# Seven RMS norms of a fused two-block kernel: from TensorE sums and transposes to VectorE sums and rows read back from memory

## The chip, the cores and the metric

The kernel runs on one core of one Trainium2 chip. The metric is device time in microseconds (us), the median of several runs. TensorE is called PE below, VectorE DVE, ScalarE ACT, GpSimd POOL, SyncE SP.

## The reference, cut to what is computed

Two blocks run one after the other on x, 512 tokens of width 1024, float32.

```
h = x
h = h + mamba2_mixer(rms_norm(h, g_pre[0]))           # SSM block
ckv, k_rope = split(rms_norm(h, g_kv_in) @ w_dkv)      # latent K/V, norm "kv"
ckv = rms_norm(ckv, g_ckv)                             # norm "ck", width 256
cq, gate = split(rms_norm(h, g_pre[1]) @ w_in)         # the same h: norm "kv" again
q = rms_norm(cq, g_q) @ w_uq                           # norm "cq", width 384
h = h + attention(q, k, v) * silu(gate) @ w_out        # 16 heads, causal
h = rms_norm(h, g_final)                               # norm "first" (sum "m1")
h = h + 0.5 * swiglu(rms_norm(h, ffn1_norm))           # norm "both" (sums "m1", "m2")
h = h + hybrid_mixer(rms_norm(h, mix_norm))            # norm "mx"
h = h + 0.5 * swiglu(rms_norm(h, ffn2_norm))           # norm "f2"
return rms_norm(h, final_norm)

rms_norm(x, g) = x * rsqrt(mean(x * x, axis=-1) + 1e-6) * g
```

A norm needs one number for each of the 512 tokens, the reciprocal root of a mean over features.

## The kernel before

Activations lie transposed: features on the 128 partitions, the 512 tokens along the row, eight tiles of 128x512 for width 1024 (`H`). Each float32 operand is split into a high part (`wr`, `XR`) and a low part (`wl`, `XL`), and each product is three matmuls (`three`, L771 to L773): of one 128x512 output tile with 1024 features, 24 matmuls. One weight load of 128x1024 is a **unit**, and mostly one unit is one output tile.

Weights flow in one fixed order of units. SP loads unit j into `raw` (4 buffers), ACT copies it to `wr` (L1221, `hi()`, 3 buffers, so it waits until PE is through with unit j-3), DVE writes the low part `wl` (L1569, `lo()`), PE begins unit j when `wl` is there. The queues of ACT and DVE are written out by hand and run in order. In the loop step of tile i, DVE first calls `lo()` for unit i+2, then does what that step has of other work, and last evicts tile i from PSUM. ACT's step i begins with `hi()` for unit i+2 and ends with the activation of what DVE evicted. So the next `hi()` stands behind this step's eviction on DVE, and the next `lo()` behind that `hi()`.

A norm is applied after the product: the weights are multiplied with the raw h times its gain, and the eviction multiplies with the row of reciprocal roots, `RS`, 128x512, the same row on every partition. The row is made so:

- ACT squares each tile of h (`square`), DVE adds the squares into `ACC` or `TB` (`fold`, L1579).
- PE sums over the partitions: `sums(key)` (L785), four matmuls of `ACC` with a column of ones, 128x4 in bank 3. It stands inside a tile, ahead of that tile's last triple.
- DVE turns the 128x4 sums into means (`root`, L1611) and takes the root by three Newton steps on 128x4 (`newton`, L1595 to L1605). For "ck" and "cq" the root is taken by POOL (L2318 to L2327).
- PE spreads the four columns into a row on all partitions: `spread(key)` (L795), four transposes of a broadcast column.
- DVE copies the row to `RS` (`row_scale`, L1618), or to `RK` for "ck" (L1916). The row of "first" is read from bank 3 where it is used.

In the attention's inputs (`latents`): 4 units `kv_down` (the last triple of one has the sum "kv"), then 11 tiles `mla_in`, steps i = 0 to 10, then 2 units for v. Step 0 evicts the two latent tiles to `craw` with `RS`, step 2 holds "ck", step 8 the sum of "cq", step 10 its row. In the first feed-forward stage (44 tiles, steps j), `fold` m1 and m2 end in step 0, both sums and both roots stand in step 1, and from `READY[0] = 3` on tiles are evicted: step 3 takes tiles 0 to 3 at once. In the second, `READY[1] = 1`. In the second mixer, `mix_v` has tokens on partitions and ACT scales by the 128x4 column `RN` (L1475); its output tiles of the second half share bank 4 with those of the first.

Of the kernel before, what the change touches and what calls it, by code (L numbers as in the profile page):

```python
# [16 lines left out]
D = 1024  # L17
# [20 lines left out]
READY = [3, 1]  # L38
# [284 lines left out]
def build_in(nc, dr, out, top):  # L323
# [28 lines left out]
    gain2 = sb("gain2", [128, KT])  # L352
    PB = [top.enter_context(nc.psum_tensor(f"pb{i}", [128, S], F32)) for i in range(8)]
# [57 lines left out]
    UPS.append([low(f"ffn1UP{i}", [128, S], F32, ph) for i in range(2)])  # L411
    ph.close()
# [28 lines left out]

    def col(name, i=0):
        at = cols[name][0] + i
        return vec[:, at:at + 1]
# [13 lines left out]
    s_sq, s_fold, s_sums, s_sv = sem("s_sq"), sem("s_fold"), sem("s_sums"), sem("s_sv")  # L458
    s_groot, s_root, s_spread, s_rs, s_vroot = [sem("s_" + n) for n in ("groot", "root", "spread", "rs", "vroot")]
# [47 lines left out]
    spreads = {n: i for i, n in enumerate(("x", "g0", "g1", "g2", "g3", "kv", "ck", "cq", "both", "first", "mix", "f2",  # L507
                                           "fin0", "fin1"))}
    sums_no = {n: i + 1 for i, n in enumerate(("x", "g0", "g1", "g2", "g3", "kv", "ck", "cq", "m1", "m2", "mx", "f2",
                                               "fin0", "fin1"))}  # L510
    rooted = {n: (s_root, i + 1) for i, n in enumerate(("x", "kv", "first", "both", "mx", "f2", "fin0", "fin1"))}
    rooted.update({n: (s_groot, i + 1) for i, n in enumerate(("g0", "g1", "g2", "g3", "ck", "cq"))})
    rooted["mix"] = rooted["mx"]
    root_of = {"both": RQ, "ck": RT, **{n: GN for n in ("g0", "g1", "g2", "g3", "cq")}}
    taken = {n: i + 1 for i, n in enumerate(("x", "g0", "g1", "g2", "g3", "kv", "ck", "cq", "m", "m2", "mx", "f2", "fin0",
                                            "fin1"))}
# [71 lines left out]
    bk.place("sum kv", 3, (s_sums, sums_no["kv"]), (s_sv, taken["kv"]))  # L588
    ring = Ring([4, 5, 6, 0, 1])
    for i, n in enumerate(MLA_ORDER):  # L590
        bk.place(("mi", n), ring.next(), whole("mla_in", n), (s_craw, 3 + n) if n < 3 else (s_sg, n - 2))
        if i == 0:
            bk.place("spread kv", 3, (s_spread, spreads["kv"] + 1), (s_rs, 2))
        if i == 2:
            bk.place("sum ck", 7, (s_sums, sums_no["ck"]), (s_sv, taken["ck"]))
        if i == 5:
            bk.place("spread ck", 7, (s_spread, spreads["ck"] + 1), (s_rk, 1))
        if i == 8:
            bk.place("sum cq", 3, (s_sums, sums_no["cq"]), (s_sv, taken["cq"]))
        if i == 10:  # L600
            bk.place("spread cq", 3, (s_spread, spreads["cq"] + 1), (s_tq, 1))
# [47 lines left out]
    def place_ffn(f):  # L649
        ring = Ring([0, 1, 2, 4, 5, 6, 7] if f == 0 else [1, 2, 4, 5, 6, 7, 0])  # L650
        name = f"ffn{f + 1}"
        for j in range(2 * FT):
            up, t = j % 2, j // 2
            bk.place((name, up, t), ring.next(), whole(name + "_in", FT * up + t),
                     (s_up if up else s_ga, FT * f + t + 1))
            if f == 0 and j == 1:
                bk.place("sum m", 3, (s_sums, sums_no["m2"]), (s_sv, taken["m2"]))
            if f == 0 and j == READY[0]:
                bk.place("spread both", 3, (s_spread, spreads["both"] + 1), (s_rs, 3))
            if f == 0 and j == READY[0] + 2:  # L660
                bk.place("spread first", 3, (s_spread, spreads["first"] + 1), (s_hn, 8))
            if f == 1 and j == 0:
                bk.place("sum f2", 3, (s_sums, sums_no["f2"]), (s_sv, taken["f2"]))
            if f == 1 and j == READY[1]:
                bk.place("spread f2", 3, (s_spread, spreads["f2"] + 1), (s_rs, 5))
# [12 lines left out]
    for hf in range(2):  # L678
        for i in range(4):
            bk.place(("vg", hf, i), ((4, 5, 6, 7), (0, 1, 2, 4))[hf][i], whole("mix_v", 4 * hf + 3),  # L680
                     (s_vg, 4 * hf + i + 1))
        if hf == 0:
            bk.place("sum mx", 3, (s_sums, sums_no["mx"]), (s_sv, taken["mx"]))
        else:
            bk.place("spread mix", 3, (s_spread, spreads["mix"] + 1), (s_rs, 4))
# [67 lines left out]
    def _(e):  # L753
# [165 lines left out]
        def latents():  # L919
            for k in range(4):  # L920
                r, l = take("kv_down", k)
                for t in (2 * k, 2 * k + 1):
                    w.wait_ge(s_xlo, tile_x(1, t))
                    for n in range(3):
                        o = opened(("kd", n)) if t == 0 else PB[n]
                        if t == 7 and n == 2:
                            sums("kv")
# [4 lines left out]
            def side(i):  # L932
                if i == 0:
                    spread("kv")
                if i == 2:
                    sums("ck")
                if i == 5:
                    spread("ck")
                if i == 8:
                    sums("cq")  # L940
                if i == 10:
                    spread("cq")

            for i, n in enumerate(MLA_ORDER):
                tile_of(("mi", n), "mla_in", n, XR, XL, ready=(s_xlo, 16), side=lambda t: side(i) if t == 7 else None)
# [120 lines left out]
        def ffn(f):  # L1066
            name = f"ffn{f + 1}"

            def side(j):
                if f == 0 and j == 1:  # L1070
                    sums("m1", 0, "m")
                    sums("m2", 4, "m")
                if f == 0 and j == READY[0]:
                    spread("both")
                if f == 0 and j == READY[0] + 2:
                    spread("first")
                if f == 1 and j == 0:
                    sums("f2")
                if f == 1 and j == READY[1]:
                    spread("f2")  # L1080

            for j in range(2 * FT):
                tile_of((name, j % 2, j // 2), name + "_in", FT * (j % 2) + j // 2, XR, XL,
                        ready=(s_xlo, 32 if f == 0 else 48), side=lambda t: side(j) if t == 7 else None)
# [64 lines left out]
        def second_mixer():  # L1149
            for hf in range(2):  # L1150
                for k in range(4):
                    r, l = take("mix_v", 4 * hf + k)
                    for t in (2 * k, 2 * k + 1):
                        c = slice(512 * (t % 2), 512 * (t % 2) + 512)
                        if t == 6 and hf == 0:
                            sums("mx")
                        if t == 6 and hf == 1:
                            spread("mix")
# [47 lines left out]
    def _(e):  # L1206
# [148 lines left out]
        def latents():  # L1355
# [11 lines left out]
            for i, n in enumerate(MLA_ORDER):  # L1367
# [7 lines left out]
                if n < 3:  # L1375
                    w.wait_ge(s_craw, 3 + n)
                    e.activation(CQ[:, 0, n, :], craw[2 + n], ACT.Copy, scale=col("g_q", n)).then_inc(s_cqhi, 1)
                    w.wait_ge(s_sums, sums_no["ck"])
# [170 lines left out]
    def _(e):  # L1549
# [40 lines left out]
        def then(sem_, last):  # L1590
            return sem_ if last else c.up()

# [271 lines left out]
        def latents():  # L1864
            for k in range(4):
# [5 lines left out]
                if k == 1:  # L1871
                    fold("kv", 7)
                if k == 3:
                    for i in range(6):
                        x_lo(2, i, H[:, i, :], col("g_pre1", i))
                    root("kv")
            for t in range(6, KT):
                x_lo(2, t, H[:, t, :], col("g_pre1", t))
            for i, n in enumerate(MLA_ORDER):
                lo()  # L1880
                if i == 0:
                    row_scale("kv")
                    w.wait_ge(s_rs, 2)
# [28 lines left out]
                if i == 2:  # L1912
                    sum_of("ck", 256)
                if i == 5:
                    w.wait_ge(*bk.full["spread ck"])
                    e.tensor_copy(RK[:, :], PB[7][:, :]).then_inc(s_rk, 1)  # L1916
                if i == 8:
                    sum_of("cq", 384)
                if i == 10:
                    w.wait_ge(*bk.full["spread cq"])  # L1920
                    w.wait_ge(s_krope, 3)
                    e.tensor_tensor(TQ[:, :], PB[3][:, :], TB[:, :], ALU.mult)
                    e.tensor_tensor(TA[64:128, :], PB[3][64:128, :], TA[64:128, :], ALU.mult)
                    e.tensor_copy(TS[96:128, :], PB[3][96:128, :]).then_inc(s_tq, 1)
# [12 lines left out]
            for hf in range(2):  # L1937
                lo()

        def project(h):  # L1940


            for kind, g, i in pieces[h + 1]:
# [19 lines left out]
                else:  # L1963
                    o = PB[bk.bank["k", g, i]]
                    w.wait_ge(*bk.full["k", g, i])
                    w.wait_ge(s_rk, 1)
# [59 lines left out]
        def ffn_side(f, j):  # L2026
# [3 lines left out]
            if f == 0 and j == 1:  # L2030
                w.wait_ge(s_sums, sums_no["m2"])
                e.tensor_scalar(SV[:, :], PB[3][:, 0:4], 1.0 / D, EPS, ALU.mult, ALU.add).then_inc(s_sv, 1)
                w.wait_ge(s_sv, taken["m"])
                newton(RN, s_root)
                w.wait_ge(*rooted["first"])
                e.tensor_tensor(RP[:, :], RN[:, :], RN[:, :], ALU.mult).then_inc(c.up(), 1)
                w.wait_ge(c.h, c.n)
                e.tensor_tensor(RP[:, :], RP[:, :], PB[3][:, 4:8], ALU.mult).then_inc(s_sv, 1)
                w.wait_ge(s_sv, taken["m2"])
                e.tensor_scalar(SV[:, :], RP[:, :], 1.0 / D, EPS, ALU.mult, ALU.add).then_inc(c.up(), 1)  # L2040
                w.wait_ge(c.h, c.n)
                newton(RQ, None)
                w.wait_ge(c.h, c.n)
                e.tensor_tensor(RQ[:, :], RQ[:, :], RN[:, :], ALU.mult).then_inc(s_root, 1)
            if f == 0 and j == READY[0]:
                row_scale("both")
            if f == 0 and READY[0] + 2 <= j < READY[0] + 6:
                w.wait_ge(*bk.full["spread first"])
                for n in (2 * (j - READY[0] - 2), 2 * (j - READY[0] - 2) + 1):
                    e.scalar_tensor_tensor(out=H[:, n, :], in0=H[:, n, :], scalar=col("g_final", n), in1=PB[3][:, :],  # L2050
                                           op0=ALU.mult, op1=ALU.mult).then_inc(s_hn, 1)
            if f == 1 and j == 0:
                fold("f2", 7)
                root("f2")
            if f == 1 and j == READY[1]:
                row_scale("f2")

        def ffn(f, gain):
            name = f"ffn{f + 1}"
            for j in range(2 * FT):  # L2060
                lo()
                ffn_side(f, j)
                for i in ffn_turn(f, j):
# [4 lines left out]
                    w.wait_ge(s_rs, 3 if f == 0 else 5)  # L2068
# [17 lines left out]
        def second_mixer():  # L2086
            for hf in range(2):
                for k in range(4):
# [3 lines left out]
                    if k == 3 and hf == 0:  # L2092
                        root("mx")
# [355 lines left out]
```

## Time and profile before

| | |
|---|---|
| median of 3 runs | 1813.01 us (1812.87 to 1813.54) |
| span of the profiled execution | 1810.9 us |
| granted TensorE clock | 0.999 |
| PE / weight loads / DVE / ACT / POOL busy | 99% / 80% / 57% / 41% / 4% |
| DMA engines busy, mean rate | about a third, 94 GB/s |

The span runs from the first to the last instruction; the time of a run has some 2 us around it. Busy shares are averages over all stages. Matmuls are pipelined, so PE's time is read from the starts of its matmuls, not from their durations.

### The profile page before, as it was taken

What the parts mean: (1) busy time and instruction counts of PE and PEld (TensorE: products, weight loads), DVE (VectorE), ACT (ScalarE), POOL (GpSimd) and SP (SyncE); (2) the same over time, 40 slices, a digit from 0 to 9 for tenths busy, and PEclk for the clock granted to TensorE, in tenths of its full rate; (3) what the DMA queues carried; (4) which work ended last, traced back from release to release, by engine and by line L of the source; (5) the groups of instructions that cost most, each with busy time, mean ns of one, the idle gap of its engine ahead of it and who ended that gap; (6) DMA issues with size and microseconds to landing.
All of it is one profiled execution on the core that took longest, in us unless ns stands there. A gap on an engine that the chain in (4) does not pass through costs nothing.

```text
span 1810.9 us, 21230 instructions
## 1 busy us (share of the span) xinstructions
PE 1799.0 (99%) x8390; PEld 1454.8 (80%) x8390; DVE 1039.5 (57%) x1502; ACT 735.5 (41%) x1202; POOL 71.1 (4%) x137
## 2 busy tenths in 40 slices
PE   9999999999999999999999999999999999999998
PEld 7777777888766788888888888888888888888887
DVE  8899986566687565444333356554444544444333
ACT  5788885433477532322222332223222322322221
POOL 1002021001210000000000000000000000000000
PEclk9999999999999999999999999999999999999999
DMA  5466562232211223333333323233333333323331
GB/s 177 93 108 112 112 107 83 98 93 93 72 36 36 82 81 105 93 93 100 93 100 101 119 81 95 95 95 102 94 98 100 94 93 102 97 93 93 102 99 56
DMA packets 50578, 170.85 MB, mean 94 GB/s; under 512 B 5808, under 2 KB 8368, under 8 KB 50480
## 3 DMA queue, kind: packets, MB, share of 16 engines
q1 hardware_dynamic: 47376, 161.44, 28.5%
q0 software_dynamic: 2240, 7.34, 4.8%
q8 instruction: 67, 1.10, 0.2%
q10 hardware_dynamic: 864, 0.72, 0.1%
q14 instruction: 31, 0.25, 0.0%
HBM read 167.31 MB, written 2.16 MB: 94 GB/s over the span
## 4 chain that ended last, share of the span: by engine, by line
PE 93%; DVE 4%; ACT 1%; issue 1%; DMA 0%; SPq 0%; DVEq 0%; ACTq 0%
PE pb L771 28%; PE pb L773 27%; PE pb L772 27%; PE pb L990 2%; PE pb L882 2%; PE pb L1019 1%; PE pb L995 1%; PE pb L1163 1%; PE pb L1165 1%; PE pb L1164 1%; PE pb L785 1%; DVE CV L1741 0%; DVE wl L1569 0%; PE pb L1173 0%; DMA raw<-in_ssm_in 0%
## 5 line engine op out<-in xcount | busy, mean ns | idle before, releaser
L771 PE MATMUL pb<-XR,wr 128*128 128x512 f32 x1584 | 625.4, 395 | 0.6 <-DVE wl L1569 0.4
L773 PE MATMUL pb<-XR,wl 128*128 128x512 f32 x1584 | 617.0, 390 | 0.0
L772 PE MATMUL pb<-XL,wr 128*128 128x512 f32 x1584 | 616.9, 389 | 0.0
L1569 DVE TENSOR_TENSOR wl<-raw,wr 128x1024 fp32r<-128x1024 f32 (+1 forms) x297 | 358.3, 1206 | 351.0 <-ACT wr L1221 349.9
L1221 ACT ACTIVATE wr<-raw 128x1024 fp32r<-128x1024 f32 (+1 forms) x295 | 305.3, 1035 | 299.1 <-PE pb L773 273.6
L771 PEld LDWEIGHTS pb<-XR,wr 128*128 128x128 f32 x1584 | 297.4, 188 | 65.8 <-issue 3.9
L773 PEld LDWEIGHTS pb<-XR,wl 128*128 128x128 f32 x1584 | 297.2, 188 | 62.6
L772 PEld LDWEIGHTS pb<-XL,wr 128*128 128x128 f32 x1584 | 297.6, 188 | 60.2 <-issue 0.2
L771 PE MATMUL pb<-ffn2HR,wr 128*128 128x512 f32 (+1 forms) x198 | 72.7, 367 | 0.0
L772 PE MATMUL pb<-ffn2HL,wr 128*128 128x512 f32 (+1 forms) x198 | 72.3, 365 | 0.0
L773 PE MATMUL pb<-ffn2HR,wl 128*128 128x512 f32 (+1 forms) x198 | 72.3, 365 | 0.0
L771 PE MATMUL pb<-ffn1HR,wr 128*128 128x512 f32 x176 | 68.5, 389 | 0.0
L772 PE MATMUL pb<-ffn1HL,wr 128*128 128x512 f32 x176 | 68.5, 389 | 0.0
L773 PE MATMUL pb<-ffn1HR,wl 128*128 128x512 f32 x176 | 68.5, 389 | 0.0
L1230 ACT ACTIVATE SQ<-H 128x512 f32<-128x512 f32 x34 | 21.5, 631 | 92.3 <-DVE H L1752 47.6
L1741 DVE SCALAR_TENSOR_TENSOR CV<-U,vec,CV 128x512 f32<-128x512 f32 x72 | 54.1, 752 | 2.5
L1460 ACT ACTIVATE ffn2HR<-ffn2UP 128x512 fp32r<-128x512 f32 x22 | 13.9, 633 | 97.1 <-DVE ffn2UP L2075 97.1
L2340 POOL TENSOR_TENSOR H<-H,RS 128x256 f32<-128x256 f32 x2 | 1.4, 730 | 1278.1 <-ACT RS L1542 1278.1
L1460 ACT ACTIVATE ffn1HR<-ffn1UP 128x512 fp32r<-128x512 f32 x22 | 13.9, 633 | 90.4 <-DVE ffn1UP L2075 90.4
L771 PE MATMUL pb<-YR,wr 128*128 128x512 f32 x128 | 50.0, 391 | 0.0
L1828 DVE TENSOR_TENSOR LL<-LL,CB 128x1024 f32<-128x1024 f32 (+1 forms) x64 | 48.4, 819 | 2.5 <-ACT LL L1290 2.5
L773 PE MATMUL pb<-YR,wl 128*128 128x512 f32 x128 | 49.8, 389 | 0.0
(354 smaller groups left out, 2317.6 us busy)
## 6 DMA issues: line engine op xcount, KB each, us to landing
raw<-in_ffn_in SPq DMA_DIRECT2D x88, 512.0 KB, 3.5
raw<-in_mix_in SPq DMA_DIRECT2D x48, 512.0 KB, 3.5
raw<-in_ssm_in SPq DMA_DIRECT2D x40, 512.0 KB, 4.3
raw<-in_ffn_out SPq DMA_DIRECT2D x32, 512.0 KB, 3.5
DB<-cum POOLq DMA_DIRECT2D x28, 256.0 KB, 8.6
raw<-in_ffn_out SPq DMA_DIRECT2D x16, 384.0 KB, 3.2
raw<-in_mla_in SPq DMA_DIRECT2D x11, 512.0 KB, 3.3
raw<-in_ssm_out_a SPq DMA_DIRECT2D x8, 512.0 KB, 3.2
```

The source lines that it names most:

```text
L771: e.matmul(o, r, xr, start=first, stop=False)
L772: e.matmul(o, r, xl, start=False, stop=False)
L773: return e.matmul(o, l, xr, start=False, stop=last)
L785: m = e.matmul(o[:, at + i:at + i + 1], accs[key][:, 128 * i:128 * i + 128], ones[:, 0:1], start=True, stop=True)
L882: m = e.matmul(y[64 * p:64 * p + 64, 128 * k:S], XD[:, k, j, 64 * p:64 * p + 64], LL[q % 2][:, p, 512 * k:512 * k + S - 128 * k], start=k ...
L990: e.matmul(o[:, at:at + n], q[:, 128 * i:128 * i + 128], kh[:, 0:n], start=True, stop=False)
L1221: e.activation(wr[j % NS][:, 0:width(j)], raw[j % NR][:, 0:width(j)], ACT.Copy).then_inc(s_hi, 1)
L1230: e.activation(SQ[i][:, :], src, ACT.Square, scale=gain).then_inc(s_sq, 1)
L1460: e.activation(HRS[f][:, t, :], UPS[f][t % 2][:, :], ACT.Copy).then_inc(s_hhi, 1)
L1569: e.tensor_tensor(wl[j % NS][:, 0:width(j)], raw[j % NR][:, 0:width(j)], wr[j % NS][:, 0:width(j)].bitcast(F32), ALU.subtract).then_inc(s_ ...
L1741: e.scalar_tensor_tensor(out=cv, in0=u[:, k:k + S], scalar=col("conv_w", 4 * ch + k), in1=cv, op0=ALU.mult, op1=ALU.add).then_inc(then(s_c ...
L1828: m = e.tensor_tensor(x, x, CB[g % 2][:, OFF[k]:OFF[k] + d].unsqueeze(1).to_broadcast([128, 2, d]), ALU.mult)
```

## The change

Seven norms ("kv", "ck", "cq", "first", "both", "mx", "f2") no longer use PE. DVE transposes `ACC` in 32x32 blocks, sums over 32, gathers the four partition groups into 32x64 and sums again: 32x16, of which partition p, column b is token 32b+p. The root is taken on this tile on DVE, a 32x32 transpose makes 16 rows of 32 tokens of it, and POOL's queue writes them (2 KB) to a scratch tensor `rows` in HBM and reads them back as a row on 128 partitions (256 KB), for "ck" and "mx" also as a 128x4 column. The norms of x, of the SSM groups and of the end stay as they were. READY[1] goes from 1 to 3.

```diff
-READY = [3, 1]
+READY = [3, 3]
+    rows = nc.dram_tensor("rows", (len(row_no), 16, 32), F32, kind="Internal").ap()
+    def row_of(key):
+        return rows[row_no[key]:row_no[key] + 1].rearrange("a b c -> a (b c)").to_broadcast([128, S])
+    def columns_of(key):
+        return rows[row_no[key]].rearrange("(c q) j -> (q j) c", q=4)
...
 # PE: latents, ffn, second_mixer
-                            sums("kv")
-            def side(i):  # sums/spread of kv, ck, cq at i = 0, 2, 5, 8, 10
-            def side(j):  # sums of m1, m2, f2; spread of both, first, f2
-                            sums("mx")
-                            spread("mix")
...
 # ACT
-                    w.wait_ge(s_groot, 5)
+                    w.wait_ge(s_cols, 16)
-                    w.wait_ge(*rooted["mx"])
+                    w.wait_ge(s_cols, 32)
...
 # DVE
+        def mean_row(key, n, scratch):
+            w.wait_ge(s_fold, sq.folded[key, sizes[key] - 1])
+            e.transpose(scratch[:, :], accs[key][:, :]).then_inc(c.up(), 1)
+            w.wait_ge(c.h, c.n)
+            e.tensor_reduce(QP[:, :], scratch[:, :].rearrange("p (b j) -> p b j", j=32), AX.X, ALU.add).then_inc(c.up(), 1)
+            w.wait_ge(c.h, c.n)
+            for q in range(4):
+                m = e.tensor_copy(scratch[0:32, 16 * q:16 * q + 16], QP[32 * q:32 * q + 32, :])
+            m.then_inc(c.up(), 1)
+            w.wait_ge(c.h, c.n)
+            e.tensor_reduce(QV[0:32, :], scratch[0:32, 0:64].rearrange("p (q b) -> p b q", q=4), AX.X,
+                            ALU.add).then_inc(s_red, 1)
+            w.wait_ge(*reduced[key])
+            if n is not None:
+                e.tensor_scalar(QV[0:32, :], QV[0:32, :], 1.0 / n, EPS, ALU.mult, ALU.add).then_inc(c.up(), 1)
+                w.wait_ge(c.h, c.n)
+        def row_root(dst):  # first guess and three Newton steps as newton(), on 32x16: 10 instructions
+        def send_row(key, src):
+            k = row_no[key]
+            if k >= 2:
+                w.wait_ge(s_rowout, 16 * (k - 1))
+            e.transpose(QT32[k % 2][0:32, :], src[0:32, :]).then_inc(s_row4, 1)
+        def row_norm(key, n):
+            mean_row(key, n, SQ[0])
+            row_root(QA)
+            send_row(key, QA)
...
                 if k == 1:
                     fold("kv", 7)
+                    row_norm("kv", D)
...
-                    row_scale("kv")
-                    w.wait_ge(s_rs, 2)
+                    w.wait_ge(*row_at["kv"])
...
                 if i == 2:
-                    sum_of("ck", 256)
+                    row_norm("ck", 256)
+                if i == 7:
+                    row_norm("cq", 384)
...
 # steps 5, 8 and 10 lose their copies; TQ, TA, TS are made behind the loop, from OT:
+            w.wait_ge(*row_at["cq"])
+            e.tensor_tensor(TQ[:, :], OT[:, :], TB[:, :], ALU.mult)
...
             if f == 0 and j == 1:
-                ... two newtons on 128x4
+                mean_row("m1", D, SQ[0])
+                row_root(QA)
+                send_row("first", QA)
+                e.tensor_tensor(QW[0:32, :], QA[0:32, 0:16], QA[0:32, 0:16], ALU.mult).then_inc(c.up(), 1)
+                mean_row("m2", None, SQ[1])
+                ... QV * QW, then the mean: two instructions
+                row_root(QB)
+                e.tensor_tensor(QB[0:32, 0:16], QB[0:32, 0:16], QA[0:32, 0:16], ALU.mult).then_inc(c.up(), 1)
+                send_row("both", QB)
-            if f == 0 and j == READY[0]:
-                row_scale("both")
...
             if f == 1 and j == 0:
                 fold("f2", 7)
-                root("f2")
+                row_norm("f2", D)
...
                     if k == 0 and hf == 0:
                         fold("mx", 7)
+                    if k == 1 and hf == 0:
+                        row_norm("mx", D)
 # POOL
+        def row_out(key):
+            k = row_no[key]
+            w.wait_ge(s_row4, k + 1)
+            e.dma_start(rows[k], QT32[k % 2][0:16, :]).then_inc(s_rowout, 16)
+        def row_in(key, dst):
+            w.wait_ge(s_rowout, 16 * row_no[key] + 16)
+            e.dma_start(dst[:, :], row_of(key)).then_inc(row_at[key][0], 16)
+        def cols_in(key, dst):
+            with nc.allow_non_contiguous_dma(reason="a column of four from a row"):
+                e.dma_start(dst[:, :], columns_of(key)).then_inc(s_cols, 16)
+        row_out("kv"); row_in("kv", RS); row_out("ck"); row_in("ck", RK); cols_in("ck", RT)
+        row_out("cq"); row_in("cq", OT)
         ... POOL's own low parts (POOL_LO)
+        row_out("first"); row_out("both"); row_in("both", RS); row_in("first", RX)
+        row_out("mx"); cols_in("mx", RN); row_in("mx", RS); row_out("f2"); row_in("f2", RS)
```

## Rows read from the trace of the kernel before

**Rows 1.** The page: PE's busy time, and the chain that ended last, by engine.
```profile
PE 1799.0 (99%) x8390; PEld 1454.8 (80%) x8390; DVE 1039.5 (57%) x1502; ACT 735.5 (41%) x1202; POOL 71.1 (4%) x137
...
PE 93%; DVE 4%; ACT 1%; issue 1%; DMA 0%; SPq 0%; DVEq 0%; ACTq 0%
```

**Rows 2.** Timeline of PE at "kv": start us, us, engine, line, instruction.
```profile
397.49 0.39 PE L773 MATMUL pb<-XR,wl 128*128 128x512 f32 x1
...
398.53 0.48 PE L771 MATMUL pb<-XR,wr 128*128 128x512 f32 x1
398.85 0.39 PE L772 MATMUL pb<-XL,wr 128*128 128x512 f32 x1
...
403.19 0.39 PE L773 MATMUL pb<-XR,wl 128*128 128x512 f32 x1
403.72 0.50 PE L771 MATMUL pb<-XR,wr 128*128 128x512 f32 x1
...
404.29 0.40 PE L773 MATMUL pb<-XR,wl 128*128 128x512 f32 x1
...
404.88 0.47 PE L771 MATMUL pb<-XR,wr 128*128 128x512 f32 x1
```

**Rows 3.** Grouped by form, DVE: the nearest shapes to the new instructions.
```profile
L1984 DVE TENSOR_REDUCE st<-pb 128x1 f32<-128x512 f32 x16 | 11.1, 692 | 4.1 <-PE pb L991 3.8
...
L1794 DVE COPY TB<-SZ 32x128 f32<-32x128 f32 x4 | 0.9, 221 | 0.1
```

**Rows 4.** Timeline of DVE: the roots of ffn1, first and last of 25 instructions.
```profile
645.05 0.16 DVE L2032 TENSOR_SCALAR SV<-pb 128x4 f32<-128x4 f32 x1 [0.67 <-PE pb L785]
...
649.79 0.16 DVE L2044 TENSOR_TENSOR RQ<-RQ,RN 128x4 f32<-128x4 f32 x1
```

**Rows 5.** DMA issues on SP's queue: count, KB, median us to landing.
```profile
BB<-in_sgu_b SPq DMA_DIRECT2D x1, 512.0 KB, 4.6
...
cum<-CM SPq DMA_DIRECT2D x1, 64.0 KB, 1.5
```

**Rows 6.** The 28 loads of DB, 256 KB each, on POOL's queue.
```profile
DMA to landing us min/median/max: 7.9/8.6/11.4
```

**Rows 7.** Timeline of DVE in the attention's inputs, from "kv" to step 4.
```profile
388.26 0.68 DVE L1579 TENSOR_TENSOR ACC<-ACC,SQ 128x512 f32<-128x512 f32 x1
...
396.91 4.06 DVE L1587 SCALAR_TENSOR_TENSOR XL<-H,vec,XR 128x512 fp32r<-128x512 f32 x6
...
406.10 0.69 DVE L1886 TENSOR_TENSOR PP<-pb,RS 128x512 f32<-128x512 f32 x1
...
426.08 1.23 DVE L1569 TENSOR_TENSOR wl<-raw,wr 128x1024 fp32r<-128x1024 f32 x1 [1.72 <-ACT wr L1221]
...
432.30 1.23 DVE L1569 TENSOR_TENSOR wl<-raw,wr 128x1024 fp32r<-128x1024 f32 x1 [1.72 <-ACT wr L1221]
```

**Rows 8.** Timeline of PE: first matmuls of tiles 5, 6 (mla_in), 6 (ffn1).
```profile
428.39 0.39 PE L771 MATMUL pb<-XR,wr 128*128 128x512 f32 x1
...
434.29 0.39 PE L771 MATMUL pb<-XR,wr 128*128 128x512 f32 x1
...
668.36 0.39 PE L771 MATMUL pb<-XR,wr 128*128 128x512 f32 x1
```

**Rows 9.** Timeline of DVE in ffn1: steps 1, 3 and 4.
```profile
643.15 1.22 DVE L1569 TENSOR_TENSOR wl<-raw,wr 128x1024 fp32r<-128x1024 f32 x1
...
656.51 0.69 DVE L1618 COPY RS<-pb 128x512 f32<-128x512 f32 x1 [2.73 <-PE pb L795]
...
664.64 1.23 DVE L1569 TENSOR_TENSOR wl<-raw,wr 128x1024 fp32r<-128x1024 f32 x1 [0.33 <-ACT wr L1221]
```

**Rows 10.** Timeline of POOL: one instruction of the root of "ck".
```profile
426.24 1.12 POOL L2322 TENSOR_TENSOR GW<-RT 128x4 f32<-128x4 f32 x1
```

**Rows 11.** Timelines in mix_v: DVE's second low part, ACT's first gelu.
```profile
1001.65 1.22 DVE L1569 TENSOR_TENSOR wl<-raw,wr 128x1024 fp32r<-128x1024 f32 x1 [1.83 <-ACT wr L1221]
...
1017.67 0.69 ACT L1475 ACTIVATE VG<-pb,RN 128x512 f32<-128x512 f32 x1 [0.51 <-PE pb L1165]
```

More of the change, by code:

```diff
@@ L352, in build_in @@
     gain2 = sb("gain2", [128, KT])
+    QP, QV, QS, QW = [sb(n, [128, 16]) for n in ("QP", "QV", "QS", "QW")]
+    QA, QB = [sb(n, [128, 32]) for n in ("QA", "QB")]
+    QT32 = [sb(f"QT32{i}", [128, 32]) for i in range(2)]
     PB = [top.enter_context(nc.psum_tensor(f"pb{i}", [128, S], F32)) for i in range(8)]
@@ L411, in build_in @@
     UPS.append([low(f"ffn1UP{i}", [128, S], F32, ph) for i in range(2)])
+    RX = low("RX", [128, S], F32, ph)
     ph.close()
@@ L440, in build_in @@
     cum = nc.dram_tensor("cum", (1, 4, 32, 128), F32, kind="Internal").ap()
+    row_no = {n: i for i, n in enumerate(("kv", "ck", "cq", "first", "both", "mx", "f2"))}
+    rows = nc.dram_tensor("rows", (len(row_no), 16, 32), F32, kind="Internal").ap()
[3 more added lines that the diff above has]
+        return rows[row_no[key]].rearrange("(c q) j -> (q j) c", q=4)
     def col(name, i=0):
@@ L458, in build_in @@
     s_sq, s_fold, s_sums, s_sv = sem("s_sq"), sem("s_fold"), sem("s_sums"), sem("s_sv")
+    s_red, s_row4, s_rowout, s_rows, s_cols = [sem("s_" + n) for n in ("red", "row4", "rowout", "rows", "cols")]
+    s_rowx = sem("s_rowx")
     s_groot, s_root, s_spread, s_rs, s_vroot = [sem("s_" + n) for n in ("groot", "root", "spread", "rs", "vroot")]
@@ L506, in build_in @@
     conv_no = {n: i for i, n in enumerate(convs)}
[L507 to L516, printed above, removed]
+    spreads = {n: i for i, n in enumerate(("x", "g0", "g1", "g2", "g3", "fin0", "fin1"))}
+    sums_no = {n: i + 1 for i, n in enumerate(("x", "g0", "g1", "g2", "g3", "fin0", "fin1"))}
+    rooted = {n: (s_root, i + 1) for i, n in enumerate(("x", "fin0", "fin1"))}
+    rooted.update({n: (s_groot, i + 1) for i, n in enumerate(("g0", "g1", "g2", "g3"))})
+    root_of = {n: GN for n in ("g0", "g1", "g2", "g3")}
+    taken = {n: i + 1 for i, n in enumerate(("x", "g0", "g1", "g2", "g3", "fin0", "fin1"))}
+    reduced = {n: (s_red, i + 1) for i, n in enumerate(("kv", "ck", "cq", "m1", "m2", "mx", "f2"))}
+    row_at = {n: (s_rows, 16 * i + 16) for i, n in enumerate(("kv", "ck", "cq", "both", "mx", "f2"))}
+    row_at["first"] = (s_rowx, 16)
     def whole(name, n):
@@ L655, in place_ffn @@
                      (s_up if up else s_ga, FT * f + t + 1))
-            if f == 0 and j == 1:
-                bk.place("sum m", 3, (s_sums, sums_no["m2"]), (s_sv, taken["m2"]))
-            if f == 0 and j == READY[0]:
[L659 to L665, printed above, removed]
         for c in range(KT if f == 0 else KT - 1):
@@ L930, in latents @@
                 m.then_inc(s_unit, 1)
-            def side(i):
[L933 to L945, printed above, removed]
+            for n in MLA_ORDER:
+                tile_of(("mi", n), "mla_in", n, XR, XL, ready=(s_xlo, 16))
             w.wait_ge(s_cklo, 2)
@@ L1067, in ffn @@
             name = f"ffn{f + 1}"
-            def side(j):
[L1070 to L1080, printed above, removed]
             for j in range(2 * FT):
                 tile_of((name, j % 2, j // 2), name + "_in", FT * (j % 2) + j // 2, XR, XL,
-                        ready=(s_xlo, 32 if f == 0 else 48), side=lambda t: side(j) if t == 7 else None)
+                        ready=(s_xlo, 32 if f == 0 else 48))
             for c in range(KT if f == 0 else KT - 1):
@@ L2067, in ffn @@
                     w.wait_ge(*bk.full[name, up, t])
-                    w.wait_ge(s_rs, 3 if f == 0 else 5)
+                    w.wait_ge(*row_at["both" if f == 0 else "f2"])
                     if not up:
@@ L2181, in _ @@
         e.memset(RQ[:, :], 0.0).then_inc(s_warm, 1)
+        for q in (QA, QB):
+            e.memset(q[:, :], 0.0).then_inc(c.up(), 1)
         for i in range(2):
@@ L2334, in _ @@
                             wr[j % NS][:, 0:width(j)].bitcast(F32), ALU.subtract).then_inc(s_lo, 1)
+        row_out("first")
+        row_out("both")
+        row_in("both", RS)
+        row_in("first", RX)
+        row_out("mx")
+        w.wait_ge(s_rowout, 16 * row_no["mx"] + 16)
+        cols_in("mx", RN)
+        row_in("mx", RS)
+        row_out("f2")
+        row_in("f2", RS)
         w.wait_ge(s_prescale, len(POOL_OUT))
```

86 lines of the change are left out of this document (32 added, 54 removed).

## The prediction, made before the changed kernel was run

> **What bounds the kernel now.** I read the page first. PE is busy for 99% of the span and makes up 93% of the chain that ended last; DVE has 4% of it [rows 1]. So the time falls by what PE no longer does, and rises by each stretch in which PE waits. Three things have then to be found: what a sum and a spread cost PE, how long the new work holds DVE, and by how much DVE may be late before PE runs dry. The first is in the timeline of PE, where the starts of matmuls have to be looked at: in an undisturbed tile they are 0.227 us apart (tile 6 starts 5.90 us behind tile 5, less 0.45 for the spread between them, over 24 [rows 8]). The last is in the timeline of DVE beside the first matmul of each tile: `lo()` for unit i+2 is called in step i and has to end before tile i+2 begins.
>
> **What PE is spared.** At "kv" the matmul ahead of the sum starts at 397.49 and the one behind it at 398.53: 1.04, less the usual 0.23, is 0.81. The next comes 0.32 later and not 0.23, another 0.09 [rows 2]. A sum costs 0.90. The spread: 404.29 to 404.88 is 0.59, less 0.23 is 0.36, with the same 0.09 behind it 0.45. There are seven sums and seven spreads: 6.3 + 3.15. And PE waits once for the low parts XL, which stand behind the root of "kv" on DVE: 403.19 to 403.72 is 0.53, 0.30 too many [rows 2]; with the root gone from there this wait goes. Together 9.8 us.
>
> **What one norm costs DVE.** No row shows a DVE transpose. Below, it can't be under the fixed part of a small instruction, 0.16 [rows 4]; above, two passes would be twice the 0.69 of a 128x512 reduction [rows 3]. It moves the same 128x512 as that reduction, so I take 0.69. The reduction of the transposed tile reads as much as L1984: 0.69. Each has some 0.03 behind it for the wait on its own result. The four copies of 32x16 are at most 0.22 each, which is what 32x128 takes [rows 3], and at least some 0.06: I take 0.12, together 0.5. The 32x64 reduction 0.23. Dependent instructions on 128x4 follow each other at (649.79 - 645.05)/24 = 0.1975 [rows 4], and 32x16 is hardly more: mean 0.2, ten for the root 1.98, last transpose 0.2. **R = 4.55 us** in all; with the transpose and copies at their bounds 3.9 to 5.6. For "first" and "both" the chain is two partition sums (2.17 each), two roots (1.98 each) and seven small instructions (1.4): **C = 9.7 us**, 8.4 to 12.
>
> **What the way through memory takes.** L is the time from the end of DVE's last transpose until the row has landed. The nearest row for reading it back is DB, 256 KB from a few addresses onto 128 partitions through the same queue: 7.9 to 11.4 [rows 6]. BB, one 4 KB row to 128 partitions from SP, 512 KB, took 4.6 [rows 5]. Writing 2 KB is at least the 1.5 of cum [rows 5]. Our 256 KB from 2 KB lie between half of BB and DB. I take 5.0 for the read and 2.2 for the write: **L = 7.2 us**, from 4.5 (1.5 and something over half of BB) to 14 (the slowest DB and 2.6). POOL also shares something with DVE: an instruction on 128x4 which otherwise takes 0.20 took 1.12, from 426.24 to 427.36 [rows 10], while DVE ran `lo()` from 426.08 to 427.31 [rows 7]. Behind the end of C, DVE runs two `lo()`; that part of L is in my 2.2 with 0.5. The Trainium skill, page "SBUF — State Buffer", section "SBUF: two separate sides", says that two SBUF inputs shut POOL out only where POOL's instruction reads SBUF, and that the descriptors of POOL's DMAs are held up by the performance modes of DVE. By that, those 0.5 us fall away and the sum below comes out 0.5 lower; the stretched instruction in the trace reads SBUF and agrees with the first half, and no row here shows the second.
>
> **Where the norm "ck" stands: step 2 of the attention's inputs.** First, DVE is earlier than before. In the new kernel "kv" is done behind its fold, from 388.9 to 393.5, in a pause of DVE, and the row lands at 393.5 + 7.2 = 400.7. The six XL end at 400.97 [rows 7], two more and one `lo()` need 0.68 x 2 + 1.23 (less overlap), and `craw` can start at 403.55 where before it was 406.10: the eleven instructions of the root and the copy to RS no longer lie between. That is 2.55 us earlier, and it is carried on, since from here ACT and DVE wait for each other and not for PE (the pause in front of `lo()` in steps 3 and 4 is one for ACT [rows 7]). Then step 2 adds R less the 0.2 of the old mean: +4.35. So `lo()` of step 4, which ended at 432.30 + 1.23 = 433.53, ends at 433.53 - 2.55 + 4.35 = 435.33. It has to be there for tile 6. That began at 434.29 [rows 8], and would now begin earlier by two sums, two spreads and the XL wait, 0.90 x 2 + 0.45 x 2 + 0.30 = 3.0, thus at 431.3. PE waits for **4.1 us** in all (3.4 of them already at tile 5: 427.31 + 1.8 = 429.1 against 428.39 - 2.55 = 425.8, two sums, a spread and the wait). What is queued behind the norm: tile 2's eviction, then ACT's SiLU of it, then ACT's high part for unit 5, then DVE's low part. Later steps have no such point: step 5 loses the copy to RK (0.7), and "cq" in step 7 delays only a `lo()` which by then has more room, because the tiles are 4 us later. The row of "cq" is sent in step 7 and used behind step 10, three tiles or 16 us later.
>
> **Where "both" stands: steps 1 to 4 of ffn1.** `lo()` of step 1 ends at 643.15 + 1.22 = 644.37 [rows 9]. C ends at 654.1, the row lands at 661.3. Before, the copy to RS ended at 657.20 and `lo()` of step 4, behind four tiles evicted in between, at 664.64 + 1.23 = 665.87 [rows 9], 8.67 later. So now 670.0. Tile 6 began at 668.36 [rows 8] and now would at 668.36 - 2 x 0.90 - 2 x 0.45 = 665.7, two sums and two spreads lying ahead of it. PE waits **4.3 us** here, some of it at tile 4, whose `lo()` stands behind C. The wait follows C + L - 12.6.
>
> **What is hidden.** "f2": its chain starts one step earlier (5.45) and is R and not C (5.15 shorter), so the row has 10 us more than that of "both", and READY of 3 is only what ffn1 has; DVE evicts from the same ring of seven banks. The price if the cover went would be that of ffn1. "mx": the chain follows `lo()` of step 1, 1001.65 + 1.22, and ends at 1007.4. ACT's first gelu began at 1017.67 [rows 11], now 0.9 earlier and 1.3 for its table ahead of it, so the column has 8 us for a write and a read of 512 pieces of 4 bytes, for which there is no row. I take it as landed in time; at DB's worst it would be late by 2.6 + 11.4 - 8 = 6 us. Both memsets at the start lie beside the first loads.
>
> **Sum.** 9.8 spared, 4.1 + 4.3 lost: 1.4 us less. The span becomes 1809.5, and the median, 2.1 above the profiled span, **1811.6 us**. A measurement of this kernel can tell some 0.2%, 3.6 us, from no change; this is within it.
>
> **Rivals.**
>
> *The row is back fast* (chance 0.22). L is 4.5, as the two DMAs of SP's queue suggest, and small instructions are cheap (R 3.9, C 8.4). For: BB moved twice the bytes in 4.6. Against: DB on this very queue never took less than 7.9. Then ffn1 waits 0.3 (8.4 + 4.5 - 12.6), "ck" 3.5: 6.0 less, 1807.0; with R and C as above and L at 4.5 it is 1.6 and 4.1, 1808.9. By the Trainium skill, page "DMA: Bandwidth & Descriptors", section "Anatomy of one DMA — SWDGE (gpsimd) path", a DMA takes 2.0 us and bytes over 436 GB/s, by estimate 2.0 + 2.6 = 4.6 for this pair, which would be this case; the rows of DB disagree by a factor of three.
>
> *The row is back late* (0.13), the one on the other side. The whole read comes from one 2 KB piece of memory, and goes like the slowest DB: L = 14. PE then waits for 9.7 + 14 - 12.6 = 11.1 in ffn1 and 4.1 at "ck", 5.4 more than is spared: 1818.4. Slower by over 0.2% it is from 13.4 us of waiting on, L above 12.2. For: DB's maximum. Against: DB is four pieces for each partition and mostly two were under way together.
>
> *No wait appears* (0.05): step 2 has room that I don't see, and L hides. Then 9.8 less, 1803.2. Against are the 1.1 us between `lo()` of step 3 and tile 5 in the trace of before.
>
> *The column of "mx" is late* (0.04): up to 6 us on top, 1817.6, the half of it within 0.2%.
>
> My own case has 0.56; alone it reaches from 1809.5 (R 3.9, L 6) to 1815.5 (C 12, L 8.8).
>
> **How the numbers follow.** Faster by over 0.2%: 0.22 + 0.05 = 0.27. Within: 0.56 + 0.02 = 0.58. Slower: 0.13 + 0.02 = 0.15. The range takes in the fast rival to its bound, 1807.0, and of the late ones the part up to 1817.5; no wait and the late row at full price are left out.
>
> **What would show it.** In the timeline of PE a hole ahead of tile 5 of mla_in (3.4) and a small one ahead of tile 6, one of about 4 us ahead of tile 6 of ffn1, none in ffn2 and mix_v; no L785 and L795 rows for these seven. In the timeline of DVE one norm of 4.5 us, and a pause ahead of the first eviction of ffn1. DB-like rows for the read with 5 us to landing. Wrong it goes if the transpose is two-pass (R, and C twice over), if L is far from 7, or if another step than 2 and 4 has the least room.

## The result, and the profile after

| | before | after |
|---|---|---|
| median | 1812.88 us (1812.37 to 1813.54, 20 runs) | 1815.38 us (1814.66 to 1816.86, 20 runs) |
| ratio | | 1.0015, 95% interval 1.0009 to 1.0021 |
| span of the profiled execution | 1810.9 us | 1813.7 us |
| granted TensorE clock, mean | 0.999 | 0.996 |

The change costs 2.5 us where 1.4 less was forecast. That is within the 0.2% that I called "no change", and within the range, but the sign is wrong and the interval excludes none. In the profiled executions it is 2.74.

The page of the changed kernel, the chain that ended last and the group of first matmuls (line, engine, operation, tiles, count, then busy us and mean ns, then idle before and its releaser):

```profile
PE 1793.9 (99%) x8306; PEld 1449.6 (80%) x8306; DVE 1057.6 (58%) x1575; ACT 736.0 (41%) x1202; POOL 71.7 (4%) x127
...
PE 90%; DVE 6%; ACT 2%; issue 1%; DMA 0%; DVEq 0%; POOL 0%; ACTq 0%; POOLq 0%
...
L760 PE MATMUL pb<-XR,wr 128*128 128x512 f32 x1584 | 626.0, 395 | 9.4 <-DVE wl L1527 9.4
```

Against [rows 1] PE has 84 instructions less, and 3% of the span went from PE's share of the chain to DVE and ACT. The last line says where: 9.4 us in which the first matmul of a tile waits for `lo()` (L1527 now). The timeline of PE has three such places. Columns are start, us, engine, line, instruction, and in brackets the idle time with what ended it:

```profile
425.26 0.39 PE L762 MATMUL pb<-XR,wl 128*128 128x512 f32 x1
429.26 0.47 PE L760 MATMUL pb<-XR,wr 128*128 128x512 f32 x1 [3.61 <-DVE wl L1527]
...
656.36 0.50 PE L760 MATMUL pb<-XR,wr 128*128 128x512 f32 x1 [0.75 <-DVE wl L1527]
...
667.14 0.39 PE L762 MATMUL pb<-XR,wl 128*128 128x512 f32 x1
672.59 0.77 PE L760 MATMUL pb<-XR,wr 128*128 128x512 f32 x1 [5.05 <-DVE wl L1527]
```

They are tile 5 of `mla_in` and tiles 4 and 6 of ffn1, which the prediction named. From start to start, less the usual 0.23, PE loses 3.77, 0.91 and 5.21: 9.9 us where 8.4 were forecast. The timeline of DVE ahead of the second and third place:

```profile
643.88 1.22 DVE L1527 TENSOR_TENSOR wl<-raw,wr 128x1024 fp32r<-128x1024 f32 x1
645.02 0.71 DVE L1554 STREAM_TRANSPOSE SQ<-ACC 128x512 f32<-128x512 f32 x1
...
655.00 0.20 DVE L1590 STREAM_TRANSPOSE QT<-QB 32x32 f32<-32x32 f32 x1
655.14 2.43 DVE L1527 TENSOR_TENSOR wl<-raw,wr 128x1024 fp32r<-128x1024 f32 x2
663.90 0.69 DVE L2065 TENSOR_TENSOR ffn1GA<-pb,RS 128x512 f32<-128x512 f32 x1 [6.33 <-DMA RS<-rows]
...
671.22 1.23 DVE L1527 TENSOR_TENSOR wl<-raw,wr 128x1024 fp32r<-128x1024 f32 x1 [0.32 <-ACT wr L1179]
```

The chain of the two norms, C, is 655.20 - 645.02 = 10.18. `lo()` for tile 6 was at 664.64 in [rows 9] and is at 671.22. POOL's queue between them (start, issue time):

```profile
655.49 0.52 POOL L2328 DMA_DIRECT2D rows<-QT  x1 [4.83 <-DVE QT L1590]
657.36 0.56 POOL L2332 DMA_DIRECT2D RS<-rows  x1 [1.36 <-DMA rows<-QT]
657.92 0.55 POOL L2332 DMA_DIRECT2D RX<-rows  x1
```

The write has landed 1.6 us after its issue, the read of "both" 6.4 after its own, beside that of "first". From DVE's last transpose to DVE's first use of the row, L, is 663.90 - 655.20 = 8.7.

So much was foreseen in kind. What was not is in the granted clock, in the stretches of PE's time around the waits (stretch, its length, busy us, matmuls, PEclk, DMA share, GB/s):

```profile
424.00:425.50 1.50, 1.50 (x8) 1.00 0.00 0
425.50:429.30 3.80, 0.19 (x2) 1.00 0.07 24
429.30:430.50 1.20, 1.20 (x6) 1.00 0.50 143
430.50:434.00 3.50, 3.50 (x10) 0.51 0.47 150
434.00:436.00 2.00, 2.00 (x11) 1.00 0.00 0
...
667.20:672.50 5.30, 0.33 (x2) 0.72 0.00 0
672.50:676.30 3.80, 3.71 (x9) 0.50 0.45 141
676.30:678.00 1.70, 1.70 (x9) 0.99 0.59 94
```

Some 1.2 us behind the first wait the clock falls to 0.51, the lower level, 1.2 GHz, and stays there for 3.5 us; in ffn1 it falls while PE still waits and stays down for 3.8 us behind it. In the timeline the starts are 0.43 apart there, not 0.227: tile 5 of `mla_in` takes 7.19 us from its first matmul to that of tile 6 (429.26 to 436.45), an undisturbed one 5.45. Thus 1.74 are lost there, and 1.8 in ffn1.

Following PE's matmuls one by one in both executions, the changed kernel is ahead by 2.88 us at tile 3 of `mla_in`, behind by 2.16 at tile 6, still behind by 0.73 as ffn1 begins, ahead by 1.11 once its two sums are past, behind by 6.05 at its tile 7, and then only gains: behind by 4.64 once `mix_v` is over and by 2.73 in ffn2. So all the loss lies at two places, and the question is whether DVE's order there and the clock are the whole cause.

### The profile page after: what moved, and what is told of

Its sections match the earlier page's. It is cut to its first block, busy times and chain, and to the rows that moved or that the text cites. A ratio compares the mean times of both kernels' runs of the same rounds, so it can differ in the third digit from the quotient of the medians.

```text
span 1813.7 us, 21118 instructions
## 1 busy us (share of the span) xinstructions
PE 1793.9 (99%) x8306; PEld 1449.6 (80%) x8306; DVE 1057.6 (58%) x1575; ACT 736.0 (41%) x1202; POOL 71.7 (4%) x127
## 4 chain that ended last, share of the span: by engine, by line
PE 90%; DVE 6%; ACT 2%; issue 1%; DMA 0%; DVEq 0%; POOL 0%; ACTq 0%; POOLq 0%
PE pb L760 27%; PE pb L762 27%; PE pb L761 27%; PE pb L965 2%; PE pb L871 2%; PE pb L994 1%; PE pb L970 1%; DVE wl L1527 1%; PE pb L1123 1%; PE pb L1122 1%; PE pb L1121 1%; ACT wr L1179 1%; DVE XL L1545 0%; DVE CV L1745 0%; PE pb L1131 0%
## 5 line engine op out<-in xcount | busy, mean ns | idle before, releaser
L1527 DVE TENSOR_TENSOR wl<-raw,wr 128x1024 fp32r<-128x1024 f32 (+1 forms) x297 | 357.9, 1205 | 343.7 <-ACT wr L1179 342.8
L761 PE MATMUL pb<-YL,wr 128*128 128x512 f32 x128 | 49.8, 389 | 0.0
```

What stands on the lines that cost most here:

```text
L761: e.matmul(o, r, xl, start=False, stop=False)
L1527: e.tensor_tensor(wl[j % NS][:, 0:width(j)], raw[j % NR][:, 0:width(j)], wr[j % NS][:, 0:width(j)].bitcast(F32), ALU.subtract).then_inc(s_ ...
```

## The experiments

Each is an edit of the changed kernel. Theory A: the place of two norms in DVE's order makes PE wait, and the waits drag the clock. Theory B: the row transfers disturb something wherever they are. Theory C: the clock falls for a reason of its own. The changed kernel is 1815.38, the kernel before was 1812.85 and 1812.88 beside these runs. In the profiled executions of `e2_evict_from_step5` and `e4_traffic` PE is already 2.5 us later at 22 us than in the changed kernel's, ahead of anything that was edited. The first tile starts 1.2 to 1.3 us later there, and the clock is at 0.50 for 3.4 us from about 9.4 us on, which costs the rest; no other profile has this. Differences read from profiles are counted from there.

**ck in the pauses.** After each eviction DVE stands 1.7 us for ACT. The norm is cut in three and put there.

```
 step 1: evict; + transpose, reduce            (ck)
 step 2: - row_norm("ck", 256)
         evict; + copies, reduce, mean         (ck)
 step 3: evict; + row_root(QA); send_row("ck", QA)
```

> The norm of ck is cut in three and put behind the evictions of steps 1, 2 and 3, where DVE stands 1.7 us for ACT's SiLU and high part. Theory A (place): the 2.5 us that the change loses come from DVE's order at two places and from the granted clock, which falls to half behind each long wait of PE. Then the wait ahead of tile 5 of mla_in (3.8 us) goes but for some tenths, and with it the 1.3 to 1.7 us of slow matmuls behind it: 5 us less than the changed kernel, about 1810.4. Theory B (memory): the row transfers disturb the weight loads or POOL, wherever DVE's norm stands: no change, 1815.4. Theory C (clock apart from waits): the wait goes, but the clock still falls: 3.8 less, 1811.6.

Measured: 1810.77 us (1808.57 to 1811.43), ratio to before 0.9986, 0.9977 to 0.9994. The median lies between the forecasts of A (1810.4) and C (1811.6); the profile tells them apart. Nothing holds PE in `mla_in`, the clock is 1.00 from 424 to 440 us, which C didn't expect, and counted from the third tile PE is 5.5 earlier at tile 6: the wait of 3.77 and the 1.74 of slow matmuls. In ffn1 the clock is down a little longer behind the wait (2.4 lost there, not 1.8), which takes some of it back. The rows are the same in number and size, so B doesn't account for this place.

**Evict from step 5.**

```
-READY = [3, 3]
+READY = [5, 3]
```

> READY of ffn1 is 5 and not 3: the low parts for tiles 6 and 7 no longer stand behind the row of both. Theory A: the wait of 5.2 us ahead of tile 6 goes, and the 1.8 us of half clock behind it; the 0.9 ahead of tile 4 stays; six evictions at 3.45 us for two end near 674.3, and the low part behind them near 675.5, ahead of tile 8: 7 us less than the changed kernel, about 1808.4. Theory B: no change, since the transfers stay as they are. Theory C: 5.2 less, 1810.2. If the six evictions are slower than I count, a new wait of up to 3 us stands ahead of tile 8.

Measured: 1809.28 us (1808.05 to 1811.27), ratio 0.9980, 0.9971 to 0.9989. The wait ahead of tile 6 is gone, the 0.9 ahead of tile 4 is there, none has come ahead of tile 8. The median again lies between A (1808.4) and C (1810.2). In the profile this place gives back 6.9, counted from the third tile, and the clock is 1.00 from 650 to 690 us: A. The eleven times fall in two groups, 1808.05 to 1809.52 and 1810.78 to 1811.27. The profiled execution, with the slow start described above, is in the second; that the start is what parts the groups fits, but is not shown.

**PE kept busy.** Matmuls without use ahead of the two long waits:

```
+for _ in range({"mla_in": 14, "ffn1_in": 20}[name]):   # only ahead of tile 5, tile 6
+    e.matmul(PB[3][:, :], xr[:, 0, 0:128], xr[:, 0, :], start=True, stop=True)
 r, l = take(name, n)                                   # waits for lo()
```

> The changed kernel, with work added: 14 matmuls into a bank that nothing uses ahead of tile 5 of mla_in and 20 ahead of tile 6 of ffn1, 3.2 and 4.5 us at 0.227 each, all inside the waits of 3.8 and 5.2. Nothing waits for their result. Theory A with the clock falling because PE stood idle: the granted clock stays at 1.0 over both places, the waits stay as they are as seen from DVE, and 1.5 to 3.5 us are saved: 1812 to 1814. Theory C: the clock falls for another reason than the pause, and the time is the same or higher, 1815.4 or more.

Measured: 1812.79 us (1812.29 to 1814.08), ratio 0.9998, 0.9989 to 1.0007: 2.6 less than the changed kernel, with 34 matmuls more. The same stretches of PE (first `mla_in`, then ffn1):

```profile
424.00:436.00 12.00, 11.09 (x48) 1.00 0.24 66
665.00:678.00 13.00, 12.99 (x58) 1.00 0.25 81
```

The clock is 1.00 throughout. DVE is as late as before the edit: the first real matmul of tile 5 starts at 429.46 (429.26 without the extra ones), and is 0.74 behind the last extra one. C falls for these two places: it is PE's standing still that costs the clock. Counted from the third tile, only 0.9 of the 1.74 come back in `mla_in`, because tile 5 now ends early enough to wait for the next `lo()` again, 0.71 ahead of tile 6; that is the second wait which the prediction had put there, and which the slow clock had hidden. In ffn1 2.2 come back, the 1.8 and a little of the wait.

**Three times the reads.**

```
 e.dma_start(dst[:, :], row_of(key))          # the row, as before
+for _ in range(2): ... e.dma_start(JUNK[:, :], row_of(key))   # 128x512 in memory
```

The added reads run one after another; those of "both" stand behind those of "first".

> The changed kernel with each row read twice more, from the same memory through the same queue into a scratch tensor in memory, behind the real read: three times the reads and some 1.8 MB more. Theory A: nothing waits for them, so 1815.4 with at most some tenths more; the wait ahead of tile 6 of ffn1 may grow if the read of first, still under way with both, slows it. Theory B: what the seven reads cost comes three times, so if the loss of 2.5 us against the kernel before is theirs, 5 us more, 1820.

Measured: 1816.13 us (1813.01 to 1817.63), ratio 1.0014, 1.0006 to 1.0023, an interval that covers that of the changed kernel. The profiled execution was the slowest of the eleven, 1817.63; counted from the third tile it is 0.35 us shorter than the changed kernel's. The three waits are 3.99, 1.13 and 5.24 from start to start, against 4.00, 1.14 and 5.44. B falls; 5 us more were its forecast.

**ck behind the eviction.** Only two things of step 2 change places.

```
 if i == 2:
-    row_norm("ck", 256)
     evict tile 2
+    row_norm("ck", 256)
```

> Only the order of two things in step 2: the eviction of the third tile first, the norm of ck whole behind it. ACT's SiLU and high part for the next unit (1.7 us) then lie beside the norm (4.85). Theory A: the low part for tile 5 comes 1.7 us earlier, the wait ahead of tile 5 is 2.1 and not 3.8, the step behind it has half a us more of room, and the clock loses less: 1.7 to 3.4 less than the changed kernel, 1812.0 to 1813.7. If the bound were the length of the norm on DVE alone and not ACT's place behind it: 1815.4.

Measured: 1813.08 us (1811.94 to 1814.84), ratio 1.0002, 0.9993 to 1.0010. The stretches of PE, the wait ahead of tile 5, that ahead of tile 6, and the long one in ffn1:

```profile
425.30:427.20 1.90, 0.24 (x3) 1.00 0.00 0
427.20:429.00 1.80, 1.80 (x8) 1.00 0.53 147
...
432.70:433.60 0.90, 0.20 (x1) 1.00 0.00 0
...
664.50:669.60 5.10, 0.32 (x2) 0.73 0.00 0
669.60:673.30 3.70, 3.69 (x9) 0.50 0.45 142
```

The first pause is 2.05 from start to start, and the clock stays at 1.00; the 1.10 ahead of tile 6 shows again. The two waits are 1.8 and 0.9, 1.1 less than the single one, and the other 1.7 of the 2.8 that it gives in the profile (2.3 in the medians) come from the clock. The wait ahead of `lo()` was thus ACT's chain behind the eviction, not the length of the norm alone.

**both in two.** The second half of the chain goes to step 2, behind `lo()` for tile 4.

```
 if f == 0 and j == 1:  m1, root, row of "first"
+if f == 0 and j == 2:
     m2, root, row of "both"
```

> The chain of first and both is cut at its middle: the sum of m1, its root and the row of first in step 1 of ffn1, m2 and the row of both in step 2, behind the low part for tile 4. Theory A: the wait of 0.9 ahead of tile 4 goes, but the row of both comes some 1.2 later, so that the wait ahead of tile 6 is as long as the row is later: unchanged at the end, 1815.4 within 0.5 (tile 6 has READY 3). A rule of mere length of the chain: 0.9 less, 1814.5.

Measured: 1815.18 us (1812.66 to 1816.07), ratio 1.0011, 1.0002 to 1.0020. The wait ahead of tile 4 is gone, that ahead of tile 6 has grown from 5.44 to 5.79 from start to start. So 0.55 less is waited in all: the wait grew by 0.35 and not by 1.2, because the row came back faster (below). But the slow matmuls behind it take 2.3 there instead of 1.8, and 0.3 is left in the profile. The interval, 1813.2 to 1816.5 when put on 1812.88, has room for both forecasts (1815.4 and 1814.5); that the row itself is what is late is seen in the timeline alone.

**first read later.** The two reads one after the other.

```
 row_in("both", RS)
+w.wait_ge(*row_at["both"])
 row_in("first", RX)
```

> The row of first is read only when that of both has landed; in the changed kernel the two reads of 256 KB are issued 0.56 us apart and are under way together, 6.45 and 7.0 us. Theory: they share what limits them, and the read of both alone takes 3.3 to 5.0 as the reads of kv and ck do. Then L falls from 8.6 to 5.5 to 7.2, the wait ahead of tile 6 from 5.2 to 2.1 to 3.7, and with the clock 1.5 to 4.5 less: 1811 to 1814. Rival: the read is slow on its own or by the weight loads beside it: 6.45 again, 1815.4.

Measured: 1814.97 us (1813.28 to 1816.20), ratio 1.0009, 1.0000 to 1.0018. The DMA of 657 to 667 us here. The first line is the queue of the weight loads (packets, MB, share of the 16 engines), the others are issues, with KB and us to landing:

```profile
q1 hardware_dynamic: 288, 1.05, 38.7%
RS<-rows POOLq DMA_DIRECT2D x1, 256.0 KB, 5.6
RX<-rows POOLq DMA_DIRECT2D x1, 256.0 KB, 3.3
```

Both theories were partly wrong. The read of "both" takes 0.8 less (6.4 to 5.6), not 1.4 to 3.1; the rest stays with it when it is alone on its queue. That one read slows another is seen in `e4_traffic` too: the row of "kv", with one more read issued 0.6 behind it, took 6.3 instead of 5.4. Beside the read here lie two weight loads, 1.05 MB. In `e6_both_in_two` the two reads are issued together as in the changed kernel (658.44 and 658.99), but only one load, 0.52 MB, lies beside them:

```profile
q1 hardware_dynamic: 144, 0.52, 17.1%
RS<-rows POOLq DMA_DIRECT2D x1, 256.0 KB, 4.6
RX<-rows POOLq DMA_DIRECT2D x1, 256.0 KB, 4.7
```

With one weight load less, the same pair of reads takes 4.6 and 4.7 instead of 6.4 and 7.0. One weight load less takes off 1.8, one read less 0.8. That the weight loads are all of the rest is argued, also from RK, which takes 3.3 with 0.28 MB beside it; no run was made to take them away. The wait ahead of tile 6 follows the row: 4.61 from start to start against 5.44. In the profile, counted from the third tile, PE is 1.0 earlier behind it; the medians are 0.4 apart, and their intervals hold either.

**All.** `e1`, `e2` and `e6` together.

> Three edits together: ck in the pauses of steps 1 to 3, READY of ffn1 at 5, the chain of first and both cut at its middle. Theory A: no wait of PE is left in mla_in and ffn1, no stretch of half clock, and the seven sums and spreads are all gain: 5.0 for ck, 6.9 for READY, 0.9 for tile 4, 1802.5, which is 10.4 below the kernel before, 0.57%. The low part for tile 8, behind six evictions, comes some 1.2 later than with READY alone and may take back up to 1 us. Theory B would leave at least 2 us of loss somewhere else: 1805 or more.

Measured: 1802.34 us (1802.08 to 1802.91), ratio 0.9942, 0.9930 to 0.9955: 10.5 less than before, 13.0 less than the changed kernel. PE in `mla_in` and in ffn1, and the group of first matmuls for the whole span:

```profile
424.00:440.00 16.00, 16.00 (x72) 1.00 0.38 117
650.00:680.00 30.00, 30.00 (x134) 1.00 0.32 106
```

```profile
L760 PE MATMUL pb<-XR,wr 128*128 128x512 f32 x1584 | 624.3, 394 | 0.6 <-DVE wl L1527 0.6
```

9.4 us of waiting have become 0.6 at one place, ahead of the first tile of the kernel (8.4 us), where the kernel before waits 0.4 too. Nothing of the price is left, so this kernel measures what the seven norms gave PE: 10.6 by the drift between the two profiles, against 9.8 forecast. The loss of up to 1 us ahead of tile 8 didn't come: its `lo()` stands behind the six evictions, from 670.19 to 671.42, and the tile begins at 671.98, so 0.6 of room is left there.

## Why the prediction was wrong

| step | forecast | measured |
|---|---|---|
| PE spared | 9.8 | 10.6 |
| R, one norm on DVE | 4.55 | 4.85 |
| C, first and both | 9.7 | 10.18 |
| L, row out and back | 7.2 | 8.7 |
| waits in `mla_in` | 4.1 | 3.8, and 0.7 more once the clock is kept |
| waits in ffn1 | 4.3 | 0.9 + 5.2 = 6.1 |
| clock | not in the sum | 1.7 + 1.8 = 3.5 |
| net | -1.4 | +2.8 |

*The step that failed* is the sum itself: "9.8 spared, 4.1 + 4.3 lost". It priced a wait of PE at its own length and put nothing for the clock. Each long wait also costs what the slower matmuls behind it take, and `e3_pe_kept_busy` shows it with the waits left in place: 2.6 us come back, as much as the whole loss, by nothing but a busy PE. With 3.5 in the sum the net would have been +2.1, and the sign right; with everything else as measured and no clock it would have been -0.7, and the sign as forecast. No row of the kernel before could have priced it. Its trace does show the clock falling, to 0.50 from 1806.6 us on, when PE's last matmul began at 1805.4, but nothing comes behind it there. It wasn't among the unknowns, and that the time lies in the range is luck: the own case reached 1815.5 only with a C of 12 that did not come (10.18), and the rest of the range was the late rival's.

*What PE is spared* was low by 0.8. Sums and spreads cost the 0.90 and 0.45 of [rows 2]; the rest is a wait of 0.5 that the kernel before had ahead of the sum of "f2" (1443.14 to 1444.68 between two matmuls), and 0.3 that I can't place.

*R and C.* The transpose of 128x512 took 0.71 and the reduction 0.69, as taken. The four copies were 0.69, 0.2 more than taken, and the 32x64 reduction 0.26. The two-pass transpose, which would have meant C of 12, is out.

*L* was low by 1.5. The write was as taken (0.3 to the issue, 1.6, 0.3 to the read's issue). The read was 6.4, not 5.0: in `e7_first_later`, without the second read under way, it was 5.6, and in `e6_both_in_two`, with one weight load less, 4.6. The prediction counted neither, though the diff issues both reads in a row. Here the estimate from the Trainium skill, page "DMA: Bandwidth & Descriptors", section "Anatomy of one DMA — SWDGE (gpsimd) path", 2.0 us and the bytes over 436 GB/s, gives 2.6 for a read; in the changed kernel the fastest of seven took 3.3 and the slowest 7.0, so the trace does not agree. For the pair, write and read, it was 1.6 + 6.4 = 8.0 against the 4.6 estimated there. The row-back-fast rival that it stood beside is out. Whether 0.5 of the way is POOL's sharing with DVE, as the prediction had it, no run shows.

*The formula for ffn1*, C + L - 12.6, was right: 10.18 + 8.7 - 12.6 = 6.3 against 6.1 measured. In `e7_first_later` L is 663.79 - 655.91 = 7.9 and it gives 5.5 against 0.9 + 4.4; in `e6_both_in_two` C is 11.3 and L 6.9, and it gives 5.6 against 5.56. So the 1.8 too little there is 0.5 of C and 1.5 of L, less 0.2 by which the formula is too high.

*"ck" in step 2* was right in place and in kind: `craw` started at 403.24 (403.55 forecast), and PE waited for 3.8 at tile 5 (3.4 forecast). What I listed as queued behind the norm, tile 2's eviction, SiLU, high part, low part, is the wait: `e5_ck_behind_evict` takes just this out and the wait falls from 3.8 to 1.8.

*Hidden ones.* "f2" and "mx" make no wait. The column of "mx" landed at 1020.42, 2.6 after its issue and 2.8 for the write ahead of it; ACT loaded its table behind it for 1.28 and then waited 1.01 more for PE, to 1022.78. So it held, with 1.0 of room.

*Small slips.* Added up again, the wait for "ck" is 435.33 - 431.3 = 4.0 and that at tile 5 429.1 - 425.8 = 3.3, not 4.1 and 3.4; the lower bounds of R and C come to 3.8 and 8.1, not 3.9 and 8.4. The bounds of the own case took C and not R to its end: with R 3.9, C 8.4 and L 6 the sum gives 1808.5, with R 5.6, C 12 and L 8.8 it gives 1816.6. None of this changes the sign.

*The rivals.* The late row was right in sign and wrong in cause: L was 8.7, not 14. No wait appears: waits appeared. The loss came by none of them.

## What to carry to other kernels

A wait of an engine that is otherwise full has two prices: its length, and the clock behind it; where a change brings one long wait, price the slow stretch as well (1.7 to 2.4 us for each of the waits of 4 us and more here). Splitting the wait in two helped once, in `e5_ck_behind_evict`; work without use during the wait helped at both places. Moving sums off the bound engine was worth its full 0.6% here, but only after the receiving engine's order was redone: put the pieces of a moved chain where that engine already stands waiting, and behind what another engine is waiting for. And a constant such as READY that was tuned to the old latency has to be set again for the new one.

## What the hardware showed that I had not expected

In `mla_in` and ffn1 the granted clock fell to 0.50 behind or within pauses of PE of 4.00, 4.61, 5.04, 5.18, 5.24, 5.44 and 5.79 us (start to start), and stayed at 1.00 behind pauses of 0.74, 1.10, 1.14 and 2.05. After the 4.00 the first 1.2 us of matmuls still ran at 1.00 and then 3.5 us at 0.51; after the 5.44 it was down from the start. In the changed kernel it was back at 1.00 4.7 us behind the first matmul after the first of these waits, and 3.7 behind the other.

The length of a pause does not decide alone. In the first 10 us of the kernel, where PE idles 0.96 and then 0.59 us in `e2_evict_from_step5` and 0.86 and 0.57 in `e4_traffic`, the clock fell to 0.50 for 3.4 us; in `e7_first_later`, with 1.41 and 0.53 at the same places, it stayed at 1.00. Why is open. With the later start of the first tile it made those two executions 2.5 us longer at 22 us, so the spans of two single profiles can't be compared without looking at their first tiles.

A 256 KB row read from one 2 KB piece of memory to 128 partitions, on POOL's queue, took 3.3 to 7.0 us in the changed kernel, by what lay beside it, and up to 7.9 in `e2_evict_from_step5`; the write of 2 KB took 1.6 in six of seven cases (2.8 in the other).
